# The scan's triangular inverse in a two-block kernel: its levels as 32x32 tiles on TensorE instead of 64x64

## What is computed

```python
def wkv_scan(r, w, k, v, kk, a, s0, reverse):
    def step(s, inp):
        r_t, w_t, k_t, v_t, kk_t, a_t = inp
        sa = jnp.einsum('bhij,bhj->bhi', s, -kk_t)
        s = (s * w_t[:, :, None, :] + sa[..., None] * (kk_t * a_t)[:, :, None, :]
             + v_t[..., None] * k_t[:, :, None, :])
        return s, jnp.einsum('bhij,bhj->bhi', s, r_t)
```

## Time and profile before

| what | value |
|---|---|
| runs, us | 2913.37, 2916.79, 2918.89 |
| span of the profiled execution, us | 2911.3 |
| median of the runs less that span, us | 5.5 |
| TensorE busy, matmul instructions | 98%, 24219 |
| VectorE, ScalarE, GpSimd busy | 65%, 46%, 9% |
| the scan's place in the span | about 460 to 940 us |
| mean granted TensorE clock of the span | 0.993 |

### The profile page before, as it was taken

How to read it: one execution, slowest core, us unless ns; L and a number is a source line. 1 busy time by engine, 2 the same in 40 slices (tenths; PEclk the granted TensorE clock), 3 DMA queues, 4 the chain that set the end, 5 groups by cost and what they waited for, 6 DMA issues and landing times.

```text
span 2911.3 us, 56972 instructions
## 1 busy us (share of the span) xinstructions
PE 2851.3 (98%) x24219; PEld 2412.6 (83%) x24219; DVE 1886.4 (65%) x2597; ACT 1341.5 (46%) x1915; POOL 248.1 (9%) x303
## 2 busy tenths in 40 slices
PE   6999999999999999999999999999999999999998
PEld 3687888988888878888888888888888888888887
DVE  3597876787887766664445657789875555554444
ACT  3222446565564444444444444566544444444443
POOL 1000002343422000000000000133100000000000
PEclk8999999999999999999999999999999999999999
DMA  9997880000000668875665656666556666666564
GB/s 386 371 380 241 277 274 27 8 8 13 8 8 19 208 201 259 263 247 174 191 189 185 195 189 209 189 183 177 172 185 194 188 189 189 190 188 201 187 194 159
DMA packets 470782, 532.31 MB, mean 183 GB/s; under 512 B 22920, under 2 KB 422722, under 8 KB 469634
## 3 DMA queue, kind: packets, MB, share of 16 engines
q1 hardware_dynamic: 464754, 516.13, 55.0%
q0 software_dynamic: 3408, 10.42, 1.1%
q10 hardware_dynamic: 2368, 2.11, 0.3%
HBM read 522.29 MB, written 4.19 MB: 181 GB/s over the span
## 4 chain that ended last, share of the span: by engine, by line
PE 92%; DVE 4%; DMA 2%; issue 1%; ACT 1%; SPq 0%; DVEq 0%; ACTq 0%
PE ps L2455 14%; PE ps L2466 14%; PE ps L2468 14%; PE ps L2467 14%; PE ps L2626 10%; PE ps L2456 7%; PE ps L2938 4%; PE ps L2939 2%; PE ps L2477 2%; PE ps L2479 2%; PE ps L2478 2%; DMA raw<-in_w_mod 1%; PE ps L2649 1%; PE ps L2527 1%; PE ps L2636 1%
## 5 line engine op out<-in xcount | busy, mean ns | idle before, releaser
L1567 DVE TENSOR_TENSOR lo<-raw,hi 128x1024 fp32r<-128x1024 f32 x776 | 948.1, 1228 | 724.3 <-ACT hi L1055 719.0
L1055 ACT ACTIVATE hi<-raw 128x1024 fp32r<-128x1024 f32 x776 | 820.2, 1059 | 1083.1 <-PE ps L2468 605.5
L2466 PE MATMUL ps<-hi,mov 128*128 128x512 f32 x1408 | 553.5, 393 | 3.7 <-DVE mov L1635 3.7
L2468 PE MATMUL ps<-hi,mov 128*128 128x512 f32 x1408 | 549.8, 391 | 0.0
L2467 PE MATMUL ps<-lo,mov 128*128 128x512 f32 x1408 | 549.4, 390 | 0.0
L2466 PEld LDWEIGHTS ps<-hi,mov 128*128 128x128 f32 x1408 | 265.2, 188 | 58.1 <-issue 4.0
L2468 PEld LDWEIGHTS ps<-hi,mov 128*128 128x128 f32 x1408 | 265.0, 188 | 55.9
L2467 PEld LDWEIGHTS ps<-lo,mov 128*128 128x128 f32 x1408 | 265.2, 188 | 54.0
L2455 PE MATMUL ps<-mov,hi 128*128 128x512 f32 x864 | 307.5, 399 | 0.4 <-DVE mov L2385 0.3
L2455 PE MATMUL ps<-hid,hi 128*128 128x512 f32 x704 | 244.3, 394 | 0.0
L2456 PE MATMUL ps<-mov,lo 128*128 128x256 f32 x864 | 243.9, 282 | 0.0
(11 more groups left out here) (436 smaller groups left out, 4281.4 us busy)
## 6 DMA issues: line engine op xcount, KB each, us to landing
raw<-in_w_in SPq DMA_DIRECT2D x184, 512.0 KB, 4.7
raw<-in_w_gate SPq DMA_DIRECT2D x176, 256.0 KB, 2.9
raw<-in_w_up SPq DMA_DIRECT2D x176, 256.0 KB, 3.2
raw<-in_w_down SPq DMA_DIRECT2D x88, 512.0 KB, 3.4
raw<-in_w_ffn_gate SPq DMA_DIRECT2D x176, 256.0 KB, 2.9
raw<-in_w_ffn_up SPq DMA_DIRECT2D x176, 256.0 KB, 3.1
raw<-in_w_ffn_down SPq DMA_DIRECT2D x88, 512.0 KB, 3.9
raw<-in_w_out SPq DMA_DIRECT2D x64, 512.0 KB, 4.2
```

The costliest lines, as they stand in the source:

```text
L1055: act.activation(hi[:, s, :, :], src, ACT.Copy).then_inc(hi_ready, 1)
L1567: dve.tensor_tensor(lo[:, s, :, :], raw_at(ph, i, j)[0], hi[:, s, :, :].bitcast(F32), ALU.subtract)\
L2466: pe.matmul(out, x(k)[:, 0, tokens], w_hi, start=first, stop=False)
L2468: mm = pe.matmul(out, x(k)[:, 1, tokens], w_hi, start=False, stop=last)
```

## The change

The inverse's blocks up to size 32 lie on the diagonal of each 64x64 block, so only 32 of the 64 columns of a row can be other than zero. The change keeps just those: per chunk and direction X, Y and XT become three tiles of 128 partitions x 4 chunks x 32 columns (`XH`, `YH`, `XTH`), laid into the memory of XY.

- Level 0: "E0" and "X0" form 1 - LEV[0] in two steps of half the columns, since one half of LEV[0]'s columns holds each row's entries; "T0" transposes half the columns.
- Levels 1 to 4: a new helper `blocks` in place of `each`. For every chunk and head it issues two matmuls, one per diagonal 32x32 block, with 32 columns, on the array tile of the same 32 rows and columns. The ScalarE copy, the VectorE subtraction and the transpose have 32 columns per chunk.
- Level 5: only the one off-diagonal block is left. Y5 takes U itself (its block that joins the halves) and so one matmul per chunk and head, on an off-diagonal array tile; T5 likewise one. VectorE first writes XTH to XT as 64 columns with the foreign half zero ("XD", `spread_halves`) and then adds the off-diagonal block ("XT", `joined`), with a column of -1 and 0 as the scalar.
- GpSimd makes five masks and not six. k_scan gets 98 columns more.

Everything from Z on reads XT as before. `in_bank(bank, SUB, 0, SUB)` reads 4 x 32 columns.

```diff
--- before.py
+++ after.py
@@ -47,6 +47,12 @@
 BANK = 512
 C = 64
 NC = T // C
+SUB = C // 2
+
+
+def into(d):
+
+    return d
 
 
 STREAM = [
@@ -253,7 +259,11 @@
             size *= 2
         scan += row + [np.concatenate([before | (s == t)] * 2, 0)]
     first = np.tile((np.arange(NC * (C + 1)) % (C + 1) != 0).astype(f), (P, 1))
-    scan = np.concatenate(scan + [first, two(np.eye(C)), two(np.eye(HEAD) - 1 / HEAD)], 1).astype(f)
+    half_of = np.arange(P)[:, None] // SUB % 2
+    own_half = (half_of == np.arange(C)[None, :] // SUB).astype(f)
+    minus_in = np.concatenate([-(half_of == into(d)).astype(f) for d in range(2)], 1)
+    eye32 = np.tile(np.eye(SUB), (P // SUB, 1))
+    scan = np.concatenate(scan + [first, two(np.eye(C)), two(np.eye(HEAD) - 1 / HEAD), own_half, eye32, minus_in], 1).astype(f)
 
 
     half = P // 2
@@ -419,13 +429,17 @@
         return [at(f"{name}{d}", offset + d * step, shape) for d in range(2)]
 
     PITCH = C + 1
-    kscan = at("kscan", R + 40 * KIB, [P, 2 * SCAN_DIR + NC * PITCH + C + HEAD])
+    HALVES = 2 * SCAN_DIR + NC * PITCH + C + HEAD
+    kscan = at("kscan", R + 40 * KIB, [P, HALVES + C + SUB + 2])
     strict = [kscan[:, d * SCAN_DIR:d * SCAN_DIR + C] for d in range(2)]
     level = [[kscan[:, d * SCAN_DIR + (1 + n) * C:d * SCAN_DIR + (2 + n) * C] for n in range(LEVELS)] for d in range(2)]
     upto = [kscan[:, d * SCAN_DIR + (1 + LEVELS) * C:(d + 1) * SCAN_DIR] for d in range(2)]
     inside = kscan[:, 2 * SCAN_DIR:2 * SCAN_DIR + NC * PITCH]
     eye64 = kscan[:, 2 * SCAN_DIR + NC * PITCH:2 * SCAN_DIR + NC * PITCH + C]
-    less_mean64 = kscan[:, 2 * SCAN_DIR + NC * PITCH + C:]
+    less_mean64 = kscan[:, 2 * SCAN_DIR + NC * PITCH + C:HALVES]
+    own_half = kscan[:, HALVES:HALVES + C]
+    eye32 = kscan[:, HALVES + C:HALVES + C + SUB]
+    minus_in = kscan[:, HALVES + C + SUB:]
     S0 = R + 49 * KIB
     stV = at("stV", S0, [P, NC, C])
     tokV = at("tokV", S0 + 2048, [P, NC, C])
@@ -465,6 +479,9 @@
     stA2, stB2, stK2 = ([of_both(q, first, width) for q in range(2)] for first, width in ((0, 2 * C), (768, C), (1280, C)))
     stA, stB, stK = ([[x[q][:, d] for d in range(2)] for q in range(2)] for x in (stA2, stB2, stK2))
     XT, AT, BM = stB, U, stK
+    halves = [[XY[d][:, :, :, :].rearrange("p c z n -> p (c z n)")[:, n * NC * SUB:(n + 1) * NC * SUB].rearrange("p (c t) -> p c t", c=NC)
+               for n in range(3)] for d in range(2)]
+    XH, YH, XTH = ([halves[d][n] for d in range(2)] for n in range(3))
     bcol = lcol[:, 6, 0:4]
 
 
@@ -499,14 +516,14 @@
         return ["U", "oA", "oB", "Yb1", "Yb2", "Yb3", "oMV", "Yb4", "Yb5", "Z"]
 
     def dve_names(q, d):
-        out = (["Q", "R"] if q else []) + ["M", "oK"] + (["oV"] if d == 0 else []) + ["X0", "T0"]
+        out = (["Q", "R"] if q else []) + ["M", "oK"] + (["oV"] if d == 0 else []) + ["E0", "X0", "T0"]
         for l in range(1, LEVELS):
-            out += [f"T{l}"] + ([f"X{l}"] if l < LEVELS - 1 else [])
+            out += [f"T{l}", f"X{l}"] if l < LEVELS - 1 else ["XD", "XT"]
         out += ["AT"] + (["rho2"] if q else []) + ["Bm"] + (["Y0"] if q else [])
         return out + [f"s{n}" for n in range(1 - q, NC - q)]
 
     def pool_names(q, d):
-        return [f"m{l}" for l in range(LEVELS)]
+        return [f"m{l}" for l in range(LEVELS - 1)]
 
     front_pe, front_act, front_dve = (Steps(sem(k), [(q, n) for q in range(2) for n in names(q)]) for k, names in (
         ("front_pe", front_pe_names), ("front_act", front_act_names), ("front_dve", front_dve_names)))
@@ -953,7 +970,7 @@
             pool.dma_start(kscan[:, :], A["k_scan"]).then_inc(kscan_in, 16)
 
             def mask_levels(b, q, gate_of=None):
-                for l in range(LEVELS):
+                for l in range(LEVELS - 1):
                     for d in range(2):
                         if l == 0:
                             scan_act[d].wait(pool, (q, "U"), b)
@@ -1293,7 +1310,7 @@
                 for l in FRONT:
                     for d in range(2):
                         scan_pe[d].wait(act, (q, f"Y{l}"), b)
-                        scan_act[d].done(act.activation(XY[d][:, :, 1, :], in_bank(4 * d + 2, C, 0, C), ACT.Copy), (q, f"Yb{l}"))
+                        scan_act[d].done(act.activation(YH[d], in_bank(4 * d + 2, SUB, 0, SUB), ACT.Copy), (q, f"Yb{l}"))
                     for d in range(2 if l == 3 else 0):
                         scan_pe[d].wait(act, (q, "MV"), b)
                         scan_act[d].done(act.activation(tokR[d][:, :, 1, :], in_bank(4 * d + 3, C, 0, C), ACT.Copy), (q, "oMV"))
@@ -1990,7 +2007,20 @@
 
                 def turned(d, l):
                     own(d, f"T{l}")
-                    done(d, dve.transpose(XY[d][:, :, 0, :], XT[q][d]), f"X{l}")
+                    done(d, dve.transpose(XH[d], XTH[d]), f"X{l}")
+
+                def spread_halves(d):
+
+                    done(d, dve.tensor_tensor(XT[q][d].rearrange("p c (a n) -> p c a n", a=2),
+                                              XTH[d].rearrange("p c (a n) -> p c a n", a=1).broadcast_to([P, NC, 2, SUB]),
+                                              own_half.rearrange("p (c a n) -> p c a n", c=1, a=2).broadcast_to([P, NC, 2, SUB]), ALU.mult), "XD")
+
+                def joined(d):
+
+                    columns = XT[q][d][:, :, (1 - into(d)) * SUB:(2 - into(d)) * SUB]
+                    own(d, "XD")
+                    done(d, dve.scalar_tensor_tensor(out=columns, in0=in_bank(4 * d, SUB, 0, SUB), scalar=minus_in[:, d:d + 1], in1=columns,
+                                                     op0=ALU.mult, op1=ALU.add), "XT")
 
                 for d in range(2 if q else 0):
                     front_pe.wait(dve, (q, f"G1_{d}"), b)
@@ -2010,17 +2040,26 @@
                 for d in range(2):
                     scan_pool[d].wait(dve, (q, "m0"), b)
                     scan_pe[d].wait(dve, (q, "tB"), b)
-                    done(d, dve.tensor_tensor(XY[d][:, :, 0, :], over_chunks(eye64), LEV[0][d][:, :, :], ALU.subtract), "X0")
+                    done(d, dve.tensor_tensor(XTH[d], over_chunks(eye32), LEV[0][d][:, :, 0:SUB], ALU.subtract), "E0")
+                    own(d, "E0")
+                    done(d, dve.tensor_tensor(XH[d], XTH[d], LEV[0][d][:, :, SUB:C], ALU.subtract), "X0")
                     own(d, "X0")
-                    done(d, dve.transpose(XT[q][d], XY[d][:, :, 0, :]), "T0")
+                    done(d, dve.transpose(XTH[d], XH[d]), "T0")
                 if q == 0 and norm is not None:
                     outputs(norm)
                 if ahead:
                     front(*following(b, q), "head")
                 for l in FRONT:
                     for d in range(2):
+                        if l == LEVELS - 1:
+                            own(d, f"X{l - 1}")
+                            spread_halves(d)
+                    for d in range(2):
                         scan_pe[d].wait(dve, (q, f"T{l}"), b)
-                        done(d, dve.tensor_tensor(XT[q][d][:, :, :], XT[q][d][:, :, :], bank(d, 0), ALU.subtract), f"T{l}")
+                        if l == LEVELS - 1:
+                            joined(d)
+                        else:
+                            done(d, dve.tensor_tensor(XTH[d], XTH[d], in_bank(4 * d, SUB, 0, SUB), ALU.subtract), f"T{l}")
                     for d in range(2 if l < LEVELS - 1 else 0):
                         turned(d, l)
                     if norm is not None and l == 5:
@@ -2627,6 +2666,16 @@
                 if name:
                     sem_of.done(mm, name)
 
+            def blocks(d, name, bank, lhs, rhs, source=None, target=None):
+
+                for c in range(NC):
+                    for head in range(2):
+                        for n in range(2) if source is None else (source,):
+                            block = lambda k: slice((2 * head + k) * SUB, (2 * head + k + 1) * SUB)
+                            rows, dest = block(n), block(n if target is None else target)
+                            mm = pe.matmul(ps[dest, 4 * d + bank, c * SUB:(c + 1) * SUB], lhs(c, rows, n), rhs(c, rows), start=True, stop=True)
+                scan_pe[d].done(mm, name)
+
             def two(d, name, bank, lhs1, rhs1, lhs2, rhs2):
 
                 for c in range(NC):
@@ -2723,16 +2772,23 @@
                     rates(*following(b, q), d)
                 for l in FRONT:
                     for d in range(2):
-                        scan_pool[d].wait(pe, (q, f"m{l}"), b)
                         scan_dve[d].wait(pe, (q, f"T{l - 1}"), b)
-                        each(scan_pe[d], d, (q, f"Y{l}"), 2, lambda c, hs: LEV[l][d][hs, c, :], lambda c, hs: XT[q][d][hs, c, :])
+                        if l < LEVELS - 1:
+                            scan_pool[d].wait(pe, (q, f"m{l}"), b)
+                            blocks(d, (q, f"Y{l}"), 2, lambda c, rows, n: LEV[l][d][rows, c, n * SUB:(n + 1) * SUB], lambda c, rows: XTH[d][rows, c, :])
+                        else:
```

(9 more changed lines are left out.)

## The result

The changed kernel takes **3014.14 us** (median of 4 runs, 3014.11 to 3015.5) against 2916.11 us (2913.37 to 2918.89) for the kernel before on the same chip: a ratio of 1.0341 [1.0328, 1.0353], 98 us slower. The prediction was 2886 us and faster.

What follows compares the result with a forecast made beforehand. The scan's levels were taken as bound by one direction's latency ring over TensorE, ScalarE and VectorE, 2.47 us a level. 8 x (2.5 + 1.8) = 34 us, less a tenth: 31 saved, 2880, plus 5.5 for the median: 2886; range 2868 to 2906.

Steps and rivals of the forecast that it cites:

- E0: Added VectorE step at a unit's start, half the columns; may cost 0.3 us more beside GpSimd's mask work.
- 8 ns per instruction, four tiles at once: Y and T of levels 1 to 4: four 32x32 tiles overlap, 32/4 = 8 ns per instruction, 0.26 us a direction.
- Rival 1: Y and T groups of levels 1 to 4: instructions come no closer than 29 ns whatever the tile; 3007 us, chance 0.12.
- rival 2: Y and T: only two tiles run at once, a direction issues in 0.52 us; 2904 us, chance 0.08.
- Copies and subtractions: ScalarE and VectorE in the levels: 256 to 128 columns, 0.28 us each, 0.10 and 0.13 less.
- the head: Unit's start, three half-width steps replacing two whole: +0.1 us per direction, perhaps 0.3 more beside GpSimd.
- The walk of a unit: Level 1 to Z, following side work on each engine: 2.5 us less for q=0, 1.8 less for q=1.
- Some 8200 more instructions ... are in the 8 ns: Added matmuls and weight loads: half are loads issued beside their matmuls, so no cost beyond 8 ns per instruction.
- Granted clock 1.00: TensorE in the scan: the granted clock stays 1.00 from 463 to 910 us.
- After Z nothing changes: Rest of each unit behind Z: no change in time; the time between joined and A stays the same.
- The rival: Clock falls to 1.2 GHz in the levels: about +1.5 us a unit, 2910 or so, up to 2930; chance 0.04.
- between levels it stays denser than at 58 us: Argument against a falling clock: sparse groups got 0.50 over 58 to 66 us, and the scan's levels remain denser.

Runs made afterwards that it cites:

- the half-count kernel with the clock restored: Changed kernel with Y and T of levels 1 to 4 for two of four chunks only, plus one wide matmul behind each: 2888.8 us, ratio 0.9911.
- The kernels at half count: Changed kernel with Y and T of levels 1 to 4 for two of four chunks: 2925.14 us; with one wide matmul behind each level: 2888.8 us.
- the square: Changed kernel 3014 us; with two wide matmuls a level 2987; with Y and T for two of four chunks 2925; that plus one wide matmul 2889.

## Why the prediction was wrong

Its steps, in its own order:
- **8 ns per instruction, four tiles at once: right.** The row of 64 lasts 0.75 us. Rival 1's 29 ns and rival 2's two tiles are both refuted by that row. By the Trainium skill, "TensorEngine Tiling (Array Packing)", section Performance Considerations, about 60 cycles of overhead go with each matmul; the rows here show no such price across tiles, 8 ns an instruction against 25 (60 cycles of 2.4 GHz, an estimate from that page). On one of the four tiles an instruction still takes about 32 ns, an estimate of four times 8. (The working has a slip: 1.96 us less 0.27 is 53 ns for one of 32, not 54, which moves the 8 ns by less than one.) That rival 1 came out at 3007 is a coincidence of sums: its place was the tile, the real place is the supply.
- **Copies and subtractions: right.** The changed kernel's groups, from 463 us to the end of the scan:
```profile
L1313 ACT ACTIVATE XY<-ps 128x128 f32<-128x128 f32 x160 | 44.0, 277 | 134.2 <-PE ps L2676 132.3
...
L2062 DVE TENSOR_TENSOR XY<-XY,ps 128x128 f32<-128x128 f32 x128 | 35.0, 282 | 116.6 <-PE ps L2676 114.3
...
L2045 DVE TENSOR_TENSOR XY<-XY,lev 128x128 f32<-128x128 f32 x32 | 22.4, 699 | 1.1
...
L2043 DVE TENSOR_TENSOR XY<-kscan,lev 128x128 f32<-128x128 f32 x32 | 17.0, 530 | 3.9 <-PE ps L2665 3.6
...
L2014 DVE TENSOR_TENSOR dirs<-XY,kscan 128x256 f32<-128x256 f32 x32 | 12.1, 419 | 0.2
```
  0.28 us each, and the spread 0.42. E0 and X0 take 530 and 699 ns while GpSimd forms masks, together more than the +0.1 us per direction and the 0.3 that the head was given. It did no harm: in the half-count kernel with the clock restored the stretch from Z to the next Y1 took 16.0 and 16.4 us in nearly all units, as before. The idle column shows the turn of roles: both engines now wait for TensorE, 132 and 114 us.
- **The walk of a unit: not refuted, and not confirmed in size.** It gave 12.0 and 11.2 us; with both causes removed 12.2 and 11.3 were measured, and the time 2888.8 against 2886. That agreement is partly luck. The kernel left out half of the products, and its level-2 rings at full clock took 1.47 us (q=0) and 1.54 (q=1) without the filler; the wide matmul, which the walk doesn't have, lengthened them to about 1.8, where the walk has 1.82 for whole groups. The changed kernel itself has one level-2 ring at full clock without a transfer's boundary in it, in its last unit:
```profile
1014.99 0.75 PE L2676 MATMUL ps<-XY,lev 32*32 32x32 f32 x64
...
1017.03 0.78 PE L2676 MATMUL ps<-XY,lev 32*32 32x32 f32 x64
```
  It takes 2.04 us; the way from T to the subtraction is 0.84 where the walk has 0.52. One ring is too few for a figure, but the gain would have been smaller than forecast. What is confirmed is that ScalarE holds the middle levels and that the copies cost what was said.
- **"Some 8200 more instructions ... are in the 8 ns": this step failed.** It priced an instruction by what the array takes to run it and put no bound on how fast TensorE is given them. What the runs showed in its place: stalls in mid-group once in 256 instructions, 88 us of steps at the transfers' boundaries in the changed kernel against 1 before, 2 with half the products, and 32 when only matmuls were added to the kernel before, at full clock. The page of before had the row that would have raised the question, the instruction queue with its 192 transfers; the prediction didn't read it. In the window of the earlier trace rows 12,100 matmuls and loads in 240 us are 256 per 5.1 us, not far from the 4.0 that turned out to be the end. At a level's ring of 2.47 us, 128 instructions are already 256 per 4.9; the change asked for 256 per 1.82.
- **Granted clock 1.00, and "After Z nothing changes": failed.** The rival was named with its row, but at 0.04, and priced at 1.5 us a unit and only for MV, norm sum and Z. The reason against it ("between levels it stays denser than at 58 us") compared with one stretch and was no bound. Measured, 0.81 over the scan, of which some 222 us are at 1.2 GHz. The kernels at half count put its price at 36 us, 2.3 us a unit, with most of it behind Z: there the rest of a unit took 17.4 and 19.0 us, and 16.0 and 16.4 with the clock restored.

The range missed for the same reasons. Its lower and upper ends came from durations of instructions; no end was set by how many there are.

The Trainium skill, "Runtime: NRT & Kernel Launch", section Instruction fetch mechanics, describes blocks of 256 instructions, the next one fetched while the current one runs. The regular cuts of this trace agree. It also says that the fetch is hidden, because instructions issue more slowly than it fills; the windows of 3.95 and 3.90 us above, with about 1.3 to 2.1 us of work in each, disagree, and the measurement decides.

**Open.** Of the 4 us from one transfer to the next the transfer itself is 1.1; why the next one starts only 1.2 us after the engine resumes, and the engine only 1.4 us after a transfer has ended, is not shown. The DMA share in those windows is 0.02, so it is not the load on the transfers' engines. The supply's rate was seen only in the scan; outside it the transfers are at least 12 us apart. The exact price of the clock in the changed kernel itself is only bounded by the square (27 to 36 us, filler included; the stretches behind Z alone grew by 24). A form of levels 1 to 4 that keeps 32 columns without doubling the matmuls wasn't tried.

## What to carry to other kernels

Count instructions per stretch as well as their durations: where small tiles run several at once, the instruction stream is a resource, and a change that halves the columns and doubles the matmuls (in fp32 four queue entries for each) can take nothing off the array's time and all off the stream's. The sign is a wait for "issue" in the middle of a group, at equal distances in instructions. And before TensorE's groups are made shorter in a latency chain, price the clock for everything around the chain, not for the groups alone.

## What the runs showed of the hardware that was not expected

- TensorE's instructions come in transfers of 16 KB, 256 of them. In the scan of the kernels with 256 instructions a level they follow each other at a median of 3.9 to 4.0 us (in the changed kernel single ones at 3.4, the fastest five in a row at 3.7): 1.2 us from the end of a stall to the next transfer, 1.1 for it, 1.4 until the next stall ends. The levels of the changed kernel use one up in about half of that.
- E0 and X0, 128 columns each, take 530 and 699 ns on VectorE while GpSimd forms masks (E0 between 293 and 703), where the levels' subtraction of the same size takes 282. That GpSimd is the reason was not tested.
- 32x32 fp32 tiles down the diagonal overlap four at once even with 32 columns: 64 instructions in 0.75 us, 32 of 8 columns in 0.43.
- The granted clock fell to 0.50 in stretches of the scan with short groups and gaps between them (2.13 us of matmuls in the 3.90 us window above), and Z then took 3.68 us instead of 1.96. One wide matmul per level, otherwise useless, made the kernel at half count 36 us faster.
